# Five equal chunks of projection columns, a split wait of the value products, and tile 9's key search moved between two phases of a decoder trunk

## The reference, cut to what matters

```python
def attn_project(h, w_in, pos):
    q, k, v, qi, ki, wi = jnp.split(h @ w_in, ATTN_SPLITS, axis=-1)   # 1024, 256, 256, 512, 64, 8 = 2120 columns
    # q, k, qi, ki: rotary on the first quarter of each head of 64

def indexer_scores(qi, wi, ki, q_pos, k_pos):
    dots = jnp.einsum('bqhd,bsd->bqhs', qi, ki)                        # 8 index heads
    s = jnp.einsum('bqhs,bqh->bqs', jax.nn.relu(dots), wi * IDX_SCALE)
    return jnp.where(k_pos <= q_pos, s, -jnp.inf)

def block(args):                                                       # 128 queries at a time
    sc = indexer_scores(qib, wib, ki, q_pos, k_pos)
    _, idx = lax.top_k(sc, 256)
    return sparse_attend(qb, gather_rows(k, idx), gather_rows(v, idx), idx <= q_pos)
    # 16 query heads, 4 key and value heads of 64, softmax over the chosen keys
```

## Time and profile before

| | us |
|---|---|
| median of three executions | 5179.24 |
| lowest and highest | 5168.59, 5180.34 |
| the profiled execution | 5186.73 |
| its span, first to last instruction | 5185.0 |
| PE, DVE, ACT, POOL busy | 4402.7, 2224.2, 1892.9, 599.0 |

### The profile page before, as it was taken

How to read it: one execution, slowest core, us unless ns; L and a number is a source line. 1 busy time by engine, 2 the same in 40 slices (tenths; PEclk the granted TensorE clock), 3 DMA queues, 4 the chain that set the end, 5 groups by cost and what they waited for, 6 DMA issues and landing times. The chain is left out here.

```text
span 5185.0 us, 52824 instructions
## 1 busy us (share of the span) xinstructions
PE 4402.7 (85%) x15076; PEld 2207.3 (43%) x15077; DVE 2224.2 (43%) x5697; ACT 1892.9 (37%) x3264; POOL 599.0 (12%) x742
## 2 busy tenths in 40 slices
PE   7998886778998999988685699995999997699991
PEld 1443331223333333333234444442677775544440
DVE  1167785556555523233253401113566764610116
ACT  0145442767666633333112122221444443222223
POOL 0111011010110111111203100001000000210002
PEclk9999896789999999999787799997999998799995
DMA  8111101000000000000255777764112211568876
GB/s 296 50 46 44 35 29 67 7 11 13 15 15 5 15 20 17 19 26 29 84 190 168 294 280 287 271 238 141 54 62 74 74 41 59 195 214 289 297 268 277
DMA packets 153392, 598.19 MB, mean 115 GB/s; under 512 B 24823, under 2 KB 28791, under 8 KB 134216
## 3 DMA queue, kind: packets, MB, share of 16 engines
q1 hardware_dynamic: 105002, 426.61, 23.0%
q0 software_dynamic: 34208, 119.30, 6.6%
q10 hardware_dynamic: 13968, 49.73, 2.4%
HBM read 459.26 MB, written 136.38 MB: 115 GB/s over the span
## 5 line engine op out<-in xcount | busy, mean ns | idle before, releaser
L2536 PE MATMUL experts_ps_gu<-w_sb,experts_xT 128*128 x1504 | 677.1, 604 | 43.3 <-DMA w_sb<-moe_w_in 38.7
L1326 PE MATMUL attend_po<-attend_PT,V 128*128 128x512 f32 x1088 | 570.6, 649 | 49.4 <-ACT attend_total L1077 49.3
L760 PE MATMUL project_pj<-project_w,project_hT 128*128 128x512 f32 (+2 forms) x1360 | 543.1, 555 | 11.0 <-ACT project_hT L494 11.0
L3257 PE MATMUL recurrent_psAB<-recurrent_hT,rec_w_in_sb 128*128 128x256 f32 x2048 | 467.9, 382 | 0.8 <-ACT recurrent_hT L2933 0.8
L2536 PEld LDWEIGHTS experts_ps_gu<-w_sb,experts_xT 128*128 128x128 f32 x1504 | 284.1, 194 | 371.3 <-issue 371.3
L1067 ACT ACTIVATE attend_PT<-attend_big 128x512 f32<-128x512 f32 x544 | 294.4, 593 | 388.6 <-PE attend_big L1315 387.5
L3257 PEld LDWEIGHTS recurrent_psAB<-recurrent_hT,rec_w_in_sb 128*128 128x128 f32 x2048 | 390.5, 192 | 68.6 <-issue 17.2
L1159 DVE CUSTOM_DVE_ANT_0 attend_junk<-attend_aux,attend_hide 128x512 bf16<-128x512 f32 (+3 forms) x496 | 284.8, 614 | 270.0 <-issue 171.4
L760 PEld LDWEIGHTS project_pj<-project_w,project_hT 128*128 128x128 f32 (+1 forms) x1360 | 238.7, 196 | 296.7 <-issue 278.3
L1104 ACT ACTIVATE attend_passed<-attend_score,attend_cand 128x2048 bf16<-128x2048 f32 (+5 forms) x186 | 323.2, 1737 | 89.5 <-DVE attend_cand L1217 71.7
L2490 DVE SCALAR_TENSOR_TENSOR experts_th<-experts_th,experts_ps_gu 128x256 f32<-128x256 f32 x94 | 39.6, 422 | 736.9 <-ACT experts_th L2469 736.9
(11 more groups left out here) (582 smaller groups left out, 5789.7 us busy)
## 6 DMA issues: line engine op xcount, KB each, us to landing
w_sb<-moe_w_in SPq DMA_DIRECT2D x64, 2048.0 KB, 11.6
w_sb<-moe_w_in SPq DMA_DIRECT2D x64, 1024.0 KB, 8.5
yb_scratch<-experts_y ACTq DMA_DIRECT2D x94, 512.0 KB, 7.9
index_slab<-ada_w_in SPq DMA_DIRECT2D x12, 2048.0 KB, 12.6
hs_scratch<-route_h SPq DMA_DIRECT2D x32, 512.0 KB, 4.0
yb_scratch<-route_blank SPq DMA_DIRECT2D x32, 512.0 KB, 14.7
V<-ada_w_in SPq DMA_DIRECT2D x6, 2048.0 KB, 10.9
project_w<-attn_w_in_in SPq DMA_DIRECT2D x8, 1060.0 KB, 17.1
```

The costliest lines, as they stand in the source:

```text
L760: last = pe.matmul(pj[0:rows, (t * NCH + c) % BANKS, 0:c1 - c0], hT[:, b, k, 0:rows], w[:, k, c0:c1], start=(k == 0), stop=(k == KC - 1))
L1326: pe.matmul(po[:, n % 2, :], V1[:, b, n, :], PT[:, g % 4, :], start=(b == 0), stop=(b == S[i] // NKV - 1)).then_inc(pv_done, 1)
L2536: last = pe.matmul(ps_gu[:, u, :], xT[:, u, k, :], w1[:, bass.ds(slot, 1), k, :].rearrange("p a n -> p (a n)"), start=(k == 0), stop=(k == ...
L3257: last = pe.matmul(psAB[:, part, 0:WB], w_in[:, k, part * D + c * P:part * D + (c + 1) * P], hT[:, n // KC % 2, k, :], start=(k == 0), sto ...
```

## The change

Three things are changed in the two phases.

The chunks of columns become five of 424, so that all ten segments of a tile are equally long on PE. `NPRE` falls from 10 to 9: tile 9 is no longer searched in the projection, the segments `FIRST` and `LAST` of the seven tiles left are set anew, the ramp of the attention is tiles 6 and 8 in place of 7 and 9, and tile 9 is indexed in step 5 (tile 12) and searched in step 6 (tile 11). The wait of a value product counts only four of the eight copies for the first head of a pair, and all eight for the second. Last, `turn_queries` and `take_queries` stand in the slot that `turning_slot` gives: the last one, as before, where the step also has index work for tile i + 3, and otherwise the one after the middle.

```diff
-NPRE = 10
+NPRE = 9
...
-    CH = [(0, 512), (512, 1024), (1024, 1536), (1536, 2048), (2048, C_END)]
-    NCH, BANKS = len(CH), 3
+    NCH, BANKS = 5, 3
+    CH = [(c * C_END // NCH, (c + 1) * C_END // NCH) for c in range(NCH)]
...
-    FIRST = dict(zip(EARLY, (40, 50, 62, 72, 88, 98, 116, 126)))
-    LAST = dict(zip(EARLY, (72, 82, 98, 108, 126, 136, 156, 166)))
+    FIRST = dict(zip(EARLY, (40, 50, 62, 74, 90, 104, 120)))
+    LAST = dict(zip(EARLY, (72, 84, 100, 114, 130, 146, 166)))
...
-        RAMP = [7, 9]
+        RAMP = [6, 8]
...
+        def turning_slot(i):
+
+            return slots(i) - 1 if late(i + 3) else min(middle(i) + 1, slots(i) - 1)
...
-                    if there(i + 2):
-                        take_queries(i + 2)
+                        if s == turning_slot(i) and there(i + 2):
+                            take_queries(i + 2)
...
-                        pe.wait_ge(o_copied, 8 * (2 * i + n // 2))
+                        pe.wait_ge(o_copied, 8 * (2 * i + n // 2) - 4 * (1 - n % 2))
...
-                    if there(i + 2):
-                        turn_queries(i + 2)
+                        if s == turning_slot(i) and there(i + 2):
+                            turn_queries(i + 2)
```

## The result

The changed kernel takes 0.9853 of the time before (95% interval 0.9836 to 0.9869): 5104.97 us is the median of three of its four executions, against 5179.79 of four before (the 5179.24 above is of three). The fourth execution of the changed kernel took 9867.39 us, is left out of all ratios as a slow one, and nothing on record explains it. In a second session the ratio was 0.9853 again (0.9835 to 0.9871). By the ratio it is faster by 76 us, where 50 were forecast, and stands at 0.9853 x 5179.24 = 5103 us, just under the range, which ended at 5104. The profiled execution took 5097.31 us (span 5095.5), at the fast end of its own runs.

The account below looks back on a forecast made before the run. The prediction took DVE to bound projection tiles 6 to 13, PE the projection before and after and attention steps 4 to 6. Its terms, -50 + 6 + 23 - 16 - 13 = -50, gave 5129 us from 5179.24, range 5104 to 5158.

Parts of the forecast that it names:

- likeliest case: The forecast itself, whole kernel: 50 us less, 5129 us, with chance 0.57.
- Part 1: Projection, tiles 6 to 13: tile 9 leaving takes its work off DVE, 46 us less (bounds 23 and 58).
- Part 2: Projection: five chunks of 424 save PE 0.8 us a tile in tiles 0 to 5 and 14 to 16, 7 us.
- coupling of both engines: Projection, at tile 13: reason given for rounding -46 - 7 to -50 us.
- Part 3: Attention ramp, tiles 6 and 8: steps 0 and 1 give back 8 us, later steps cost 14, together +6.
- Part 4: Attention, steps 5 and 6: tile 9's index products and search cost +23 us (bounds 8 and 87).
- Rival (c): Attention: step 6 becomes ACT's at 8.3 us a slot, +87 in place of the search's 8; 5208 us, chance 0.04.
- Parts 5 and 6: Attention: value products wait for their own half's copies, -16 us; queries turned one slot after the middle, -13 us.
- rival (d): More gain: shorter stalls keep the clock up (10 us), four dropped slots give back whole ones (8); 5111 us, chance 0.14.
- (a): Projection: the chain of PE, ACT and DVE sets the slots, saving 25 instead of 50 us; 5154 us, chance 0.12.
- (b): Attention: early query copies stall the exponentials, +12 us; 5141 us, chance 0.08.
- (e): Tile 9's move is a wash: projection -25, attention index and search +37, in all +5 us; 5184 us, chance 0.05.

## Why the forecast fell short

The direction was right, and tile 9's move, the equal chunks and both waits each gained time by themselves. The size was 50 instead of 76 us, just beyond the edge of the range. Two steps of the prediction failed. It took tiles 14 to 16 of the projection for PE's own pace and priced a gain there at 0, where 6 to 7 us came. And its likeliest case priced PE's stalls by their length alone, where the clock that is lost behind them was worth some 14 us more (an estimate, from the clocks of steps 5 to 14). By phases of the traces:

| | before | after | change | forecast |
|---|---|---|---|---|
| projection | 692.3 | 629.7 | -62.6 | -50 |
| steps 0 and 1 | 299.6 | 295.7 | -3.9 | -8 |
| steps 2 to 15 | 1334.1 | 1317.9 | -16.2 | +8 |
| all else | 2859.0 | 2852.2 | -6.8 | 0 |

- **Part 1, tile 9's work on DVE.** Right for tiles 6 to 13 (47.4 by itself against 46). The step that failed is "then PE is nearly alone again": I read PE's busy 97.5 of 105.1 us in the earlier trace rows as PE's pace. The kernel with equal chunks shows that less PE work does not shorten this stretch, and the one with the old spans shows the same three tiles at 89.2 once DVE has 53 instead of 75 us to do. Tile 9's move took 7 us from it, priced at 0; the prediction's own table had the new plan at 40 + 30 + 30 = 100 us for these tiles, 5 less than the 105.1 of the kernel before, and did not book it. What held PE were DVE's norm and rotary, late behind the searches (12.3 of 15.3 us of PE's waits in the kernel with equal chunks), and the clock: at 0.92 over 105.1 us it lacks 8 us. DVE's sum in the stretch is not the measure: with tile 9 moved it is as busy as before (76 us against 75). Nor are ACT's rounds by themselves, which also shrank there (18 us of ACT instead of 55): in the kernel with tile 8 moved ACT has 42.7 us to do and the stretch takes 88.6. How much DVE's lateness at the end of tile 13 adds was not separated.
- **Part 2, chunks.** 8 us as a whole time, forecast 7. In its places it was less right: 4.6 in tiles 0 to 5, 3.5 in 6 to 13 where I had 0, none in 14 to 16 where I had 2.4. Against the rule that the prediction took from the Trainium skill (TensorE: Matmul & The Clock Gate, The mechanism), the gain came: a pass of 424 columns takes 0.36 us while PE never pauses. The same section of the Trainium skill also lets a load run ahead if it goes to the background weight buffer, which the prediction left out.
- The sum of the first two parts was -53 and was rounded to **-50 for the coupling of both engines**. Both kernels together gave -62.6; that deduction had no row behind it.
- **Part 3, ramp.** Forecast -8 and +14. Steps 0 and 1 gave back 3 in the kernel with tile 9 alone, no more than step 1 gives in kernels that don't touch it, and step 0 takes no less with two slots fewer. ACT's rounds fill it, and slots are nearly free there. The low bound of a slot, its exponentials, was already too much.
- **Part 4, index and search of tile 9 in the attention.** 19 us by itself, 23 forecast. The step of tile 12 grew to 135.9 us, not to about 145; that of tile 11 came to 119.0, as forecast (120). Rival (c) did not come: step 6 took 5.0 us a slot.
- **Parts 5 and 6, the waits.** Forecast -16 and -13, and -29 together. By whole times they measured -19 and -15 each by itself, and -44 together; the trace of both has the attention 50 shorter. The lengths were nearly right: of the 42 us in steps 5 to 14 some 28 are the stalls, and steps 2 to 4 lost 2 more. (The row of PE's waits fell by 40, but it overstates the split wait, 1.10 us for a gain of 0.87 in the middle of step 7.) The term that was missing is the granted clock: the earlier trace rows show 0.98 in steps 4, 6 and 7, which I had read as nearly full, but a fall of 0.02 in 105 us is 2 us a step, as much as the stall itself. I had it as rival (d), with 0.14 and with 10 us; it was part of the likeliest case. Some 3 of the 50 us are step 1, unexplained as said above.
- **Rivals.** (a) fell: the stretch lost 51.8 us, not half of it, and the spans alone are worth 19, as DVE's sums have it. (b) fell: the early queries gained 15 us by themselves. (d) was right on the clock and wrong on the slots, which gave back nothing that can be told from the spread. (e) fell with (a) and (b).

What stays open: after the attention the profiled execution is 6.2 us shorter than that of before, 0.9 in the second pair of traces. Nothing of the change is there, and traces of other kernels differ by up to 16 us in these phases, so I take it for their own spread.

## What to carry to other kernels

A phase whose work is hung on a schedule by hand can be forecast by adding each engine's work per tile and taking the larger, as long as one engine is clearly the larger (near the balance, with tile 8 moved, the table was 12 and 20 us too low). Check it against the old schedule first, and look at the stretch behind the congestion too, for here an engine that was late there still held the others. Price a stall of PE by its length and by the clock that falls behind it: a clock of 0.98 over a step of 100 us is a term of the sum, 2 us. Where an engine with slack can hold a phase's work, move the most expensive piece next; here tile 8, which brought another 0.5 to 0.7%.

## What the runs showed that I had not expected

A stall of 2.36 us on PE cost a further 1.7 us through the clock (step 8, 88.0 against 86.3 us), and products without use, put into the stalls, brought that back, though the waits ended no sooner where the timeline was read (step 7). An equally long stall in step 7 had no fall behind it, and the whole time shows no gain of these products (0.9995). Two more slots in step 0 cost nothing (131.7 against 133.3 us).
